# Moving the softmax normaliser of block 2's attention heads from VectorE to GpSimd, one pipeline step later

## The reference, cut to what matters

```
ps = masked_softmax(ls, ds >= 0)          # exp(z - max) / sum
os_ = einsum(ps, vsel)
pw = masked_softmax(lw, ...)
ow = einsum(pw, vw)
return gx[..., 0:1] * oc + gx[..., 1:2] * os_ + gx[..., 2:3] * ow
```

## Time and profile before

| | |
|---|---|
| median of 3 runs | 2070.64 us (2070.33 to 2073.42) |
| profiled execution | 2071.59 us |
| its span, first to last instruction | 2069.7 us |
| mean granted TensorE clock | 0.992 |
| busy PE / POOL / ACT / DVE | 2012.6 / 1619.6 / 1085.4 / 866.5 us |
| head loop, layer 2 | 1195.75 to 1242.9 us of the span |
| head loop, layer 3 | 1779.77 to 1826.9 us of the span |

### The profile page before, as it was taken

The page is one execution under the profiler, slowest core; times in us unless marked ns, Lnnn a source line. Parts: engine busy times, 40 slices in busy tenths (PEclk is TensorE's granted clock), DMA queues, the critical chain, the costliest instruction groups (busy, mean ns, idle before and its releaser), DMA issues.

```text
span 2069.7 us, 32431 instructions
## 1 busy us (share of the span) xinstructions
PE 2012.6 (97%) x12426; PEld 1754.1 (85%) x12426; DVE 866.5 (42%) x2030; ACT 1085.4 (52%) x2116; POOL 1619.6 (78%) x1291
## 2 busy tenths in 40 slices
PE   8999999999999999999999989999999999999997
PEld 7788999897888899898778858888997788678886
DVE  3422466066541466173323172563332412644641
ACT  3454566466245566445454585544444554865543
POOL 6495898977286798999799608899997897268997
PEclk9999999999999999999999999999999999999999
DMA  8653555553054476465446604555554467135553
GB/s 301 123 183 123 168 194 169 183 182 120 1 163 163 143 244 215 164 203 185 141 164 191 222 21 163 184 184 191 176 194 151 145 204 227 63 122 176 192 183 112
DMA packets 243470, 343.13 MB, mean 166 GB/s; under 512 B 8787, under 2 KB 171699, under 8 KB 243189
## 3 DMA queue, kind: packets, MB, share of 16 engines
q1 hardware_dynamic: 231320, 331.35, 48.7%
q10 hardware_dynamic: 11997, 9.72, 2.4%
HBM read 336.85 MB, written 4.19 MB: 165 GB/s over the span
## 4 chain that ended last, share of the span: by engine, by line
PE 83%; POOL 6%; DVE 3%; issue 3%; ACT 2%; DMA 1%; POOLq 1%; DVEq 0%; SPq 0%; ACTq 0%
PE bank L757 9%; PE bank L760 9%; PE bank L764 9%; PE bank L779 7%; PE bank L807 7%; PE bank L813 7%; PE bank L810 6%; POOL w_lo L1526 6%; PE bank L837 5%; PE bank L840 5%; PE bank L844 5%; PE bank L784 4%; DVE E L2197 1%; DVE E L2211 1%; DMA ring<-in_w_in 1%
## 5 line engine op out<-in xcount | busy, mean ns | idle before, releaser
L1526 POOL TENSOR_TENSOR w_lo<-ring,w_hi 128x512 fp32r<-128x512 f32 (+1 forms) x1216 | 1575.2, 1314 | 396.8 <-ACT w_hi L1617 359.7
L1617 ACT ACTIVATE w_hi<-ring 128x512 fp32r<-128x512 f32 (+1 forms) x1216 | 757.6, 630 | 791.0 <-PE bank L807 271.3
L757 PE MATMUL bank<-x_pair,w_hi 128*128 128x256 f32 x1504 | 381.6, 286 | 3.0 <-DVE x_pair L2112 2.3
L760 PE MATMUL bank<-x_pair,w_hi 128*128 128x256 f32 x1504 | 379.0, 284 | 0.0
L807 PE MATMUL bank<-w_hi,x_pair 128*128 128x512 f32 (+1 forms) x752 | 299.0, 398 | 2.9 <-issue 1.6
L757 PEld LDWEIGHTS bank<-x_pair,w_hi 128*128 128x128 f32 x1504 | 290.2, 193 | 5.9 <-ACT w_hi L1617 2.7
L810 PE MATMUL bank<-w_hi,x_pair 128*128 128x512 f32 (+1 forms) x752 | 292.9, 390 | 0.0
L760 PEld LDWEIGHTS bank<-x_pair,w_hi 128*128 128x128 f32 x1504 | 290.3, 193 | 0.4
L764 PE MATMUL bank<-x_pair,w_lo 128*128 128x256 f32 x1504 | 242.5, 284 | 0.0
L813 PE MATMUL bank<-w_lo,x_pair 128*128 128x512 f32 (+1 forms) x752 | 234.8, 394 | 4.2 <-POOL w_lo L1526 3.4
L764 PEld LDWEIGHTS bank<-x_pair,w_lo 128*128 128x128 f32 x1504 | 208.3, 193 | 0.0
(11 more groups left out here) (314 smaller groups left out, 2428.6 us busy)
## 6 DMA issues: line engine op xcount, KB each, us to landing
ring<-in_w_in SPq DMA_DIRECT2D x74, 1024.0 KB, 5.1
ring<-in_ffn_w_up SPq DMA_DIRECT2D x44, 1024.0 KB, 5.1
ring<-in_w_ffn_in SPq DMA_DIRECT2D x44, 1024.0 KB, 5.1
ring<-in_ffn_w_down SPq DMA_DIRECT2D x20, 1024.0 KB, 5.0
ring<-in_w_ffn_out SPq DMA_DIRECT2D x20, 1024.0 KB, 5.0
ring<-in_xattn_wkv SPq DMA_DIRECT2D x16, 1024.0 KB, 5.2
ring<-in_w_o_ret SPq DMA_DIRECT2D x16, 1024.0 KB, 5.0
ring<-in_od_w_in SPq DMA_DIRECT2D x12, 1024.0 KB, 5.1
```

The costliest lines, as they stand in the source:

```text
L757: m = mm(out_, view(w_hi)[:, k, :], x_hi[:, 4 * kh + k, :], start=start, stop=False)
L760: mm(out_, view(w_hi)[:, k, :], x_lo[:, 4 * kh + k, :], start=False, stop=False)
L1526: tt(view(w_lo), src, view(w_hi), ALU.subtract).then_inc(w_lo_ready, 1)
L1617: return A(o, i_, ACT.Copy, **kw)
```

## The change

In block 2 the pipeline gets one step more between exponentials and scaling (`lag` 2 instead of 1). In between, POOL raises four sums per partition to the power -1 (`one_over`), for each of the 16 pairs; its calls stand behind the remainders of `mb1` and in front of those of `onsa0`. DVE makes no reciprocal, no product with the gate and no drain any more: each of its four passes multiplies by two scalars of a partition, 1/sum and the gate. DVE's step becomes `maxima(s)`, `scale(s-2)`, `out(s-5)`; PE's `scores(s)`, `turn(s-3)`, `values(s-4)`; ACT's `exps(s-1)`, `probabilities(s-3)`. `E` is read as eight rows of 384 in the same memory, so that a pair's rows come round after four pairs; `sums`, `nmax` and `coef` grow to eight rows. Block 1's pairs keep their lag, reciprocal and passes by one scalar.

```diff
+        E_pairs = E[:, :, :].rearrange("p a n -> p (a n)").rearrange("p (r n) -> p r n", n=384)
...
-        sums = sb("sums", [P, 6, 2])
+        sums = sb("sums", [P, 8, 2])
...
+            nc.gpsimd.memset(minus_one[:, :], -1.0)
...
-                self.e0, self.pt0 = 2 * (ring_at % 3), 2 * (ring_at % 2)
+                self.e0, self.pt0 = 2 * (ring_at % 4), 2 * (ring_at % 2)
+                self.lag = 1 if kw["gates"] is None else 2
...
+            def one_over(pairs):
+
+                for pair in pairs:
+                    w = np.s_[:, pair.e0:pair.e0 + 2, :]
+                    pool.wait_ge(exp_ready, pair.kw["n_exp"] + 1)
+                    tt(coef[w], sums[w], minus_one[:, :].rearrange("p (a b) -> p a b", a=2), ALU.pow).then_inc(one_over_ready, 1)
...
-                remainders(f"{L}qn0", f"{L}qn1", f"{L}mb0", f"{L}vv", f"{L}mb1", f"{L}onsa0", f"{L}onsa1", f"{L}out0", f"{L}out1")
+                remainders(f"{L}qn0", f"{L}qn1", f"{L}mb0", f"{L}vv", f"{L}mb1")
+                one_over(nsa_heads(i))
+                remainders(f"{L}onsa0", f"{L}onsa1", f"{L}out0", f"{L}out1")
...
             def scale(pair):
-                c = coef[:, pair.e0:pair.e0 + 2, :]
-                dve.wait_ge(exp_ready, pair.kw["n_exp"] + 1)
-                nc.vector.reciprocal(c, sums[:, pair.e0:pair.e0 + 2, :])
-                drain()
-                if pair.kw["gates"] is not None:
-                    tt(c, c, pair.kw["gates"], ALU.mult)
+                gates = pair.kw["gates"]
+                if gates is None:
+                    dve.wait_ge(exp_ready, pair.kw["n_exp"] + 1)
+                    nc.vector.reciprocal(coef[:, pair.e0:pair.e0 + 2, :], sums[:, pair.e0:pair.e0 + 2, :])
                     drain()
-                for r in (pair.e0, pair.e0 + 1):
+                else:
+                    dve.wait_ge(one_over_ready, pair.kw["n_exp"] - len(causal_block1()) + 1)
+                for par in range(2):
+                    r = pair.e0 + par
                     for t, lo, hi in ((0, 0, P), (1, P, 384)):
-                        m = ts(E[:, r, lo:hi], E[:, r, lo:hi], coef[:, r, t:t + 1], None, ALU.mult)
+                        p = E_pairs[:, r, lo:hi]
+                        if gates is None:
+                            m = ts(p, p, coef[:, r, t:t + 1], None, ALU.mult)
+                        else:
+                            m = ts(p, p, coef[:, r, t:t + 1], gates[:, par, t:t + 1], ALU.mult, ALU.mult)
                 m.then_inc(p_ready, 1)
```

More of the change, by code:

```diff
@@ L225, in build @@
         rel = sb("rel", [BUCKETS + 1, NSA_HEADS])
-        sums = sb("sums", [P, 6, 2])
-        nmax = sb("nmax", [P, 6, 2])
-        coef = sb("coef", [P, 6, 2])
+        sums = sb("sums", [P, 8, 2])
+        nmax = sb("nmax", [P, 8, 2])
+        coef = sb("coef", [P, 8, 2])
         rstd = sb("rstd", [P, 2])
@@ L238, in build @@
         half = sb("half", [P, 8])
+        minus_one = sb("minus_one", [P, 4])
         stats = sb("stats", [P, 8, 6])
@@ L244, in build @@
         dn_g = sb("dn_g", [P, P])
-        sb("line_rest", [P, 8])
+        sb("line_rest", [P, 28])
         with ExitStack() as below:
@@ L405, in build @@
         exp_ready = sem("exp_ready")
+        one_over_ready = sem("one_over_ready")
         p_ready = sem("p_ready")
@@ L897, in heads @@
             def heads(hs, first=0):
-                n = len(hs)
-                for step in range(first, n + 3):
+                n, lag = len(hs), hs[0].lag
+                for step in range(first, n + 2 + lag):
                     if step < n:
                         scores(hs[step])
[L902 to L905, removed]
+                    if 0 <= step - 1 - lag < n:
+                        turn(hs[step - 1 - lag])
+                    if step >= 2 + lag:
+                        values(hs[step - 2 - lag])
             def scores(pair):
@@ L923, in turn @@
                     for c in range(3):
-                        m = tr(bank[b][:, c * P:(c + 1) * P], E[:, pair.e0 + par, c * P:(c + 1) * P], ident[:, :])
+                        m = tr(bank[b][:, c * P:(c + 1) * P], E_pairs[:, pair.e0 + par, c * P:(c + 1) * P], ident[:, :])
                     m.then_inc(full[b], 1)
@@ L1668, in heads @@
             def heads(hs, first=0):
-                n = len(hs)
-                for step in range(n + 2):
+                n, lag = len(hs), hs[0].lag
+                for step in range(n + 1 + lag):
                     if first <= step - 1 < n:
                         exps(hs[step - 1])
-                    if step >= 2:
-                        probabilities(hs[step - 2])
+                    if step >= 1 + lag:
+                        probabilities(hs[step - 1 - lag])
             def exps(pair):
@@ L1680, in exps @@
                     for t, lo, hi in ((0, 0, P), (1, P, 384)):
-                        m = A(E[:, r, lo:hi], E[:, r, lo:hi], ACT.Exp, bias=nmax[:, r, t:t + 1], scale=-1.0, accum_out=sums[:, r, t:t + 1])
+                        m = A(E_pairs[:, r, lo:hi], E_pairs[:, r, lo:hi], ACT.Exp, bias=nmax[:, r, t:t + 1], scale=-1.0, accum_out=sums[:, r, t:t + 1])
                 m.then_inc(exp_ready, 1)
@@ L2181, in heads @@
             def heads(hs, out, made=0):
-                n = len(hs)
-                for step in range(made, n + 4):
+                n, lag = len(hs), hs[0].lag
+                for step in range(made, n + 3 + lag):
                     if step < n:
                         maxima(hs[step])
[L2187 to L2190, removed]
+                    if 0 <= step - lag < n:
+                        scale(hs[step - lag])
+                    if step >= 3 + lag:
+                        out(hs[step - 3 - lag])
             def maxima(pair):
@@ L2196, in maxima @@
                     for t, lo, hi in ((0, 0, P), (1, P, 384)):
-                        m = nc.vector.tensor_tensor_reduce(E[:, r, lo:hi], bank[b][:, lo:hi], pair.kw["bias"][par][:, lo:hi], -1.0, 3e38,
+                        m = nc.vector.tensor_tensor_reduce(E_pairs[:, r, lo:hi], bank[b][:, lo:hi], pair.kw["bias"][par][:, lo:hi], -1.0, 3e38,
                                                            ALU.add, ALU.min, nmax[:, r, t:t + 1])
```

## The result

| | kernel before | changed kernel |
|---|---|---|
| median, range, runs | 2073.34 us (2070.33 to 2076.71), 14 | 2080.55 us (2074.22 to 2084.45), 14 |
| ratio of the times, 95% interval | | 1.003 (1.0019 to 1.004) |
| profiled execution, span | 2071.59, 2069.7 us | 2074.9, 2073.1 us |

The account below looks back on a forecast made before the run. PE, busy 97% of the span, was taken to bound the kernel. Its waits falling from 5.4 to 4.3 us a layer gain 2.3 us for both, from 2070.64 to 2068.3 us; range 2064.3 to 2072.6 us.

Parts of the forecast that it names:

- the loop: Block 2's head loops: PE's waits for DVE's scaled rows fall from 5.4 to 4.3 us a layer.
- the start: Head loop's first pairs: PE idles 1.52 and 0.55 us, together 2.07 for 1.01 before, as the first scaling comes later.
- the stores: DVE steps with a store: PE's transposes wait 0.70 us twice a layer, 1.40 for 1.96 before.
- the end: Head loop's last pairs: PE waits 0.85 us for pair 13, in place of 0.41 and 1.09.
- no 0.24: Plain steps of the head loop: PE's four waits of 0.24 us vanish, 0.96 us a layer.
- rival A: DVE's passes in the head loops: the second scalar is hidden; gain 3.0 us a layer, 2064.6 us in all; chance 0.18.
- rival C: POOL's power in the head loops: over 3.1 us, it delays scaling in all 16 pairs; 2090 us at 3.5; chance 0.05.
- rival B: Head loops: POOL's power holds DVE's passes by 0.58 or 0.15 us; 1.0 us a layer lost, 2072.6 us; chance 0.14.
- The work behind the loop is PE's and shifts whole.: After the head loop's last transpose nothing changes in order, so the gain of 2.3 us for both layers stays whole.
- the rule for two-port modes: SBUF access: a two-port DVE instruction and a GpSimd one exclude each other; the trace agreed for subtraction, not for the power.

Follow-up runs that it names:

- e6: e5 with the gates left out of DVE's pass, which then multiplies by one scalar (output lacks the gates): 2068.18 us, ratio 0.9977 to the kernel before.
- e9: e5 with POOL also multiplying the gates in after its power, and DVE's passes by one scalar, nothing left out: 2066.68 us, ratio 0.9964 to the kernel before.
- e1: Kernel before with only the padding `line_rest` grown from 8 to 40 columns, moving `region` and `hidden` 128 bytes on: 2082.25 us, ratio 1.0043.
- e2: Changed kernel with only `line_rest` taken out, so `region` and `hidden` lie where the kernel before has them: 2075.92 us, ratio 1.0004 to the kernel before.
- e5: Changed kernel with `minus_one` in the place of `line_rest`, which is gone, every old tile at its old byte: 2073.13 us, ratio 0.9998 to the kernel before.
- e10: Kernel before with a 32-column tile ahead of `ring`, moving `ring`, `x_pair`, `w_hi`, `w_lo`, `E`, `hidden` and `region` 128 bytes on: 2072.68 us, ratio 0.9996.
- e12: Kernel before with a 32-column tile between `x_pair` and `w_hi`, moving `w_hi`, `w_lo` and all behind them 128 bytes on: 2076.01 us, ratio 1.0009.
- e3: Kernel before with `line_rest` at 72 columns, moving `region` and `hidden` 256 bytes on: 2072.38 us, ratio 0.9992.
- e7: e5 with lag 1 in place of 2, POOL's power still between exponentials and scaling: 2074.78 us, ratio 1.0011 to the kernel before.
- e8: e5 with reciprocal and gate product back on DVE, passes by one scalar, no power on POOL, lag 2 kept: 2078.96 us, ratio 1.0023 to the kernel before.
- e4: Kernel before with `line_rest` at 136 columns, moving `region` and `hidden` 512 bytes on: 2072.99 us, ratio 0.9998.
- e11: Kernel before with `line_rest` at 24 columns, moving `region` and `hidden` 64 bytes on: 2082.73 us, ratio 1.0044.

## Why the prediction was wrong, step by step

**Right: the loop.** PE in the changed kernel, at the loop's start and at pair 13:

```profile
1199.46 0.93 PE L918 MATMUL bank<-region 64*128 64x128 f32 x8 [0.27 <-ACT xs L1734]
1201.61 0.87 PE L928 MATMUL bank<-ident,E 128*128 128x128 f32 x6 [1.23 <-DVE E L2230]
...
1203.88 0.87 PE L928 MATMUL bank<-ident,E 128*128 128x128 f32 x6 [0.54 <-DVE E L2230]
...
1220.80 0.87 PE L928 MATMUL bank<-ident,E 128*128 128x128 f32 x6 [0.67 <-DVE E L2230]
...
1237.72 0.87 PE L928 MATMUL bank<-ident,E 128*128 128x128 f32 x6 [0.84 <-DVE E L2230]
```

Worked out were 1.52 (measured 0.27 + 1.23) and 0.55 (0.54) at the start, 0.70 twice (0.67) for the stores, 0.85 (0.84) at the end, and no 0.24, where the earlier trace rows has four; a gain of 1.1 to 1.2 us a layer, measured 1.24 (47.13 to 45.89). DVE's passes took 407 ns for 256 columns, so rival A is refuted (its loop is e6's). The power took 1041 ns in the mean, so rival C is refuted too.

**Right: no hold by the power (rival B).** Two powers on POOL, and DVE's passes beside them, from the timelines:

```profile
1207.39 1.01 POOL L1530 TENSOR_TENSOR coef<-sums,minus_one 128x4 f32<-128x4 f32 x1 [1.49 <-ACT E L1695]
1210.05 1.11 POOL L1530 TENSOR_TENSOR coef<-sums,minus_one 128x4 f32<-128x4 f32 x1 [1.65 <-ACT E L1695]
```

```profile
1207.99 1.24 DVE L2230 TENSOR_SCALAR E<-E,coef,region 128x128 f32<-128x128 f32 x4
...
1210.45 1.25 DVE L2230 TENSOR_SCALAR E<-E,coef,region 128x128 f32<-128x128 f32 x4
```

Both groups start while a power runs, and the longest pass of the 64 in this loop took 410 ns. In e9, beside POOL's powers and products, the one-scalar passes of 256 columns took 346 ns, for the 347 of the earlier trace rows with nothing on POOL. B wanted a wait of 0.15 to 0.58 us there. The prediction tested the rule for two-port modes on L2133, which has two SBUF inputs and isn't shown to be in such a mode; it is these passes that speak against a hold, and whether they are in such a mode no run shows.

**Wrong: "The work behind the loop is PE's and shifts whole."** I followed order, waits and durations and let every matmul outside the loops keep its duration. `minus_one` and the grown padding were costed at nothing, as tiles that nobody waits for. What they moved was `hidden` against `w_hi`, and 1440 matmuls of 512 columns with weights from it took 5 ns more: 7.8 us by the stretches, and 1 us on the 192 others. The sum as it should have been: -2.5 for the loops, +8.8 for these matmuls, 6.3 us. At full clock the changed kernel stands 5.4 us over before (2059.1 and 2053.7), 0.9 from the sum, about twice the error of such a mean; the clocks of the kernel before in the result's own runs are not on record, so 2053.7 is that of the three groups. e1 gives the second term alone as 8.9 (6.4 to 11.6 by its ratio), e2 and e5 the first as 2.6 and 2.0.

What failed was the place of a tile, not a wait: e2 and e5, with the change's whole work and `hidden` back at its old byte, have 390 ns again.

The Trainium skill, SBUF — State Buffer, "Who interferes with whom", gives PE two independent read ports, one for the moving operand and one for the weights, and says that PE never waits on anyone. The durations here differ from what that suggests: the same two streams took 390 or 395 ns by their distance modulo 256 bytes. Whether the two reads of PE meet in a bank of SBUF, or in something else, no run here tells; only the dependence is shown. That the 128 bytes between the two operands matter, and not those between `hidden` and some other tile, rests on e10 and on e12, where the penalty went to the matmuls whose two operands had been moved apart.

**Not settled: the clock.** The granted clock falls to the lower level (1.2 of 2.4 GHz) for short stretches. Windows of the kernel before (stretch, its length, PE's busy time and instructions, granted clock, DMA share, GB/s):

```profile
440.00:460.00 20.00, 20.00 (x153) 0.91 0.49 158
460.00:480.00 20.00, 20.00 (x99) 0.91 0.32 106
...
1160.00:1180.00 20.00, 20.00 (x155) 0.91 0.52 160
```

and of e2:

```profile
440.00:460.00 20.00, 20.00 (x146) 0.83 0.37 123
460.00:480.00 20.00, 20.00 (x105) 0.83 0.32 106
...
1177.00:1181.00 4.00, 4.00 (x30) 0.53 0.76 253
1181.00:1185.00 4.00, 4.00 (x20) 0.61 0.03 10
```

Around 1177 PE has just run a stretch of narrow matmuls (in e2, 3.83 us of matmuls of 64x15 from 1174.44 on). What such windows cost is estimated as (1 - clock) x length: here 1.6 us more than before in each of the first two, and 0.47 x 4 + 0.39 x 4 = 3.4 for 0.09 x 20 = 1.8 in the last, 4.8 us in these three places. But it isn't e2's doing in particular: e3, which has the instructions of the kernel before, shows the same doubled stretches in its profiled execution, and e9 none at 1177. The mean clocks of the kernels lie between 0.9887 (e2) and 0.9912 (e9) and don't follow the place of tiles. Whether they follow the edit is not settled. e2, e5, e6, e7 and e8 have 0.9887, 0.9898, 0.9895, 0.9898 and 0.9892, each under the kernel before on the same chip (0.9902 or 0.9905), while e9, with the same lag, and the changed kernel have 0.9912 and 0.9904. So a gain of 2 us shows at full clock and not in the ratio, and it may be that the edit itself pays for it in clock. What sets the share of low-clock time in a run stays open.

## What to carry to other kernels

A tile added, widened or dropped moves all tiles behind it: read the addresses before and after, and if a matmul's weights and its moving operand change their distance modulo 256 bytes, cost every matmul between them (here 5 ns on 1440, three times the edit's gain), by a run with the padding alone: the sign isn't the same for every form. Put a new small tile where nothing behind it moves, as e5 does, or pad to a multiple of 256 bytes. Relieve an engine of the whole of the work and not of half: the second scalar ate half of what DVE was spared, and POOL, which had the time, could take the gate as well.

## What the runs showed that I had not expected

- 512 columns against weights in another tile: 390 ns with the weights 0, 256 and 512 bytes from their old place, 395 to 396 at 64 and 128 (L837 in e3, e4, e11, e1), 390 with both operands moved together (e10).
- A distance can also help: `x_pair` streamed, 256 columns, `w_hi` as weights, 286 ns together and 284 at 128 bytes' distance (e12); but `x_pair` against `w_lo` on L785 283 for 281.
- A two-scalar pass of 256 columns takes 407 ns and of 128 columns 342; with one scalar 347 and 281 (e6).
- A product over 128x4 on POOL took 259 ns and a power 1036 (e9) to 1041 (changed kernel).
